# Constant products on TensorE before the first tile, sums moved from VectorE to GpSimd, and gate copies placed elsewhere, in a two-block model on one core

## What is computed

```
def even_layer(h, ...):
    q, k, v, g_a, z, xbc, dt_raw = split(h @ w_in)
    y_a = rmsnorm(diff_attention(q, k, v), subln_w) * 0.8 * silu(g_a)
    xs, bm, cm = split(silu(causal_dwconv(xbc, conv_w, conv_b)))
    y = ssd_scan(xs, softplus(dt_raw + dt_bias), A, bm, cm) + xs * d_skip
    y_b = group_rmsnorm(y * silu(z), ssd_norm_w)
    return concatenate([y_a, y_b]) @ w_out

def _hybrid_mixer(u, ...):
    g = sigmoid(g_merge)                       # [.., 3, 1024]
    merged = (g[0] * (o_a @ w_up[0]) + g[1] * (o_b @ w_up[1]) + g[2] * (o_c @ w_up[2]))
    return merged @ w_out
```

## Time and profile before

| | |
|---|---|
| median of three runs | 1611.04 us |
| lowest, highest | 1607.83, 1613.50 us |
| profiled execution, its own time | 1614.3 us |
| its span in the profile | 1612.6 us |
| PE busy | 1551.4 us (96%) |
| DVE, ACT, POOL busy | 810.5, 659.5, 233.9 us |
| mean granted clock of PE | 0.987 |

### The profile page before, as it was taken

One profiled execution on the slowest core, in us unless ns is written; L12 is line 12 of the kernel. 1 busy time (PEld: TensorE's weight loads), 2 busy tenths in 40 slices (PEclk: granted clock), 3 DMA queues, 4 the chain that ended last, 5 costly groups with the idle time before them and its releaser, 6 DMA issues. The chain is left out here.

```text
span 1612.6 us, 20637 instructions
## 1 busy us (share of the span) xinstructions
PE 1551.4 (96%) x7850; PEld 1269.7 (79%) x7850; DVE 810.5 (50%) x1617; ACT 659.5 (41%) x1369; POOL 233.9 (15%) x147
## 2 busy tenths in 40 slices
PE   7999999999999999999999999999899999999998
PEld 6888777777787889878878777778777888888886
DVE  3323288757734566546524476737556333333224
ACT  4222355565523377634225544454245322322112
POOL 0000022155400012200012223122102000000000
PEclk9999999999999999999999999989999999999999
DMA  5232211111322431023521311112220323222232
GB/s 211 91 105 91 92 56 50 53 47 46 118 91 79 141 89 53 28 92 110 155 77 54 105 66 53 53 53 93 90 79 26 105 92 105 91 96 101 91 105 78
DMA packets 39777, 137.60 MB, mean 85 GB/s; under 512 B 4928, under 2 KB 5312, under 8 KB 39552
## 3 DMA queue, kind: packets, MB, share of 16 engines
q1 hardware_dynamic: 33984, 123.75, 22.9%
q10 hardware_dynamic: 5696, 12.55, 2.6%
HBM read 128.02 MB, written 2.10 MB: 81 GB/s over the span
## 5 line engine op out<-in xcount | busy, mean ns | idle before, releaser
L213 ACT ACTIVATE cut_hi<-raw 128x1024 fp32r<-128x1024 f32 x228 | 241.8, 1061 | 603.9 <-PE ps L230 594.2
L230 PE MATMUL ps<-h_hi,cut_hi 128*128 128x512 f32 (+1 forms) x1120 | 450.6, 402 | 10.6 <-DVE arena L1234 6.2
L218 DVE TENSOR_TENSOR cut_lo<-raw,cut_hi 128x1024 fp32r<-128x1024 f32 x171 | 211.3, 1235 | 461.7 <-ACT cut_hi L213 459.9
L232 PE MATMUL ps<-h_hi,cut_lo 128*128 128x512 f32 (+1 forms) x1120 | 437.0, 390 | 0.0
L231 PE MATMUL ps<-h_lo,cut_hi 128*128 128x512 f32 (+1 forms) x1120 | 436.4, 390 | 0.0
L230 PEld LDWEIGHTS ps<-h_hi,cut_hi 128*128 128x128 f32 x1120 | 211.5, 189 | 75.0 <-issue 23.6
L232 PEld LDWEIGHTS ps<-h_hi,cut_lo 128*128 128x128 f32 x1120 | 211.3, 189 | 45.1
L231 PEld LDWEIGHTS ps<-h_lo,cut_hi 128*128 128x128 f32 x1120 | 211.8, 189 | 37.4
L218 POOL TENSOR_TENSOR cut_lo<-raw,cut_hi 128x1024 fp32r<-128x1024 f32 x57 | 137.6, 2414 | 649.6 <-ACT cut_hi L213 649.6
L230 PE MATMUL ps<-cut_hi,h_hi 128*128 128x512 f32 (+1 forms) x304 | 118.3, 389 | 6.4 <-DVE cut_lo L218 5.4
L232 PE MATMUL ps<-cut_hi,h_lo 128*128 128x512 f32 (+1 forms) x304 | 117.4, 386 | 0.0
(11 more groups left out here) (348 smaller groups left out, 2199.8 us busy)
## 6 DMA issues: line engine op xcount, KB each, us to landing
raw<-weights SPq DMA_DIRECT2D x228, 512.0 KB, 3.3
scr<-scr ACTq DMA_DIRECT2D x34, 64.0 KB, 3.5
x<-x_in SPq DMA_DIRECT2D x4, 512.0 KB, 6.3
x<-x_in ACTq DMA_DIRECT2D x1, 2048.0 KB, 7.9
q_stack<-qT_lo ACTq DMA_DIRECT2D x16, 128.0 KB, 2.3
out<-x SPq DMA_DIRECT2D x4, 512.0 KB, 2.6
consts<-tables ACTq DMA_DIRECT2D x1, 1732.0 KB, 7.9
big_row<-big_in ACTq DMA_DIRECT2D x2, 512.0 KB, 7.0
```

The lines of the kernel that those rows point to most:

```text
L213: act.activation(cut_hi[:, u % CUT, :], raw[:, u % RAW, :], ACT.Copy).then_inc(hi_ready, 1)
L218: eng.tensor_tensor(cut_lo[:, u % CUT, :], raw[:, u % RAW, :], cut_hi[:, u % CUT, :].bitcast(F32), ALU.subtract).then_inc(lo_ready, 1)
L230: a = pe.matmul(out, left[0], right[0], start=start, stop=False)
L232: return a, pe.matmul(out, left[1], right[0], start=False, stop=stop)
```

## The change

Eighteen matmuls of a constant tile by itself are put in front of PE's first wait; the tile is set by DVE (the wait counts of `setup_chain` go up by one). In `Norm.dve` each tile is scaled right after its own `add_eps`. In the state-space stage seven of the eight copies of L1234 stand earlier in DVE's program: copy 0 before the copies of x, copy 1 before the scalings by dt, copies 2, 3, 5, 6 before the `mix` of their chunk, copy 7 behind one gating of `out_a` and not three; copy 4 stays. In `Up` POOL makes the last four sums too, DVE cuts the low half of `out_m`'s unit 0 and makes the low halves of tiles 0 to 3 behind the gatings 16 to 19; the high and low halves of tiles 4 to 7 go to `out_m` (new class `OutM`), behind the cuts of its unit 1.

```diff
+        warm = part(0, [P])
+
         class Setup(Part):
+            WARM = 18
...
             def pe(self, pe):
+                pe.wait_ge(setup_chain, 2)
+                for i in range(self.WARM):
+                    pe.matmul(ps[:, i % 8, 0:P], warm[:, 0:P], warm[:, 0:P], start=True, stop=True)
                 pe.wait_ge(const_loaded, 16)
 
             def dve(self, dve):
                 dve.memset(neg_half, -0.5).then_inc(setup_chain, 1)
+                dve.memset(warm, 1.0).then_inc(setup_chain, 1)
...
                 else:
-                    for t in range(self.nt + 1):
-                        if t < self.nt:
-                            self.add_eps(dve, t)
-                        if t:
-                            self.scale(dve, t - 1)
+                    for t in range(self.nt):
+                        self.add_eps(dve, t)
+                        self.scale(dve, t)
...
                 dve.tensor_tensor(pick[:, :], ident[:, 0:64], ident[:, 64:128], ALU.add)
+                gates.dve_turn(dve, 0)
                 for p, i in enumerate(TURN_ORDER):
...
-                    if p == 3:
-                        gates.dve_turn(dve, 0)
...
+                gates.dve_turn(dve, 1)
                 dve.wait_ge(*turn_out(6))
                 dve.wait_ge(*turn_out(7))
                 for t in range(NT - 1):
                     times_dt(dve, t, xdt_ready)
-                gates.dve_turn(dve, 1)
...
+                    if i in (0, 1, 4, 5):
+                        gates.dve_turn(dve, 2 + (0, 1, 2, 4, 5).index(i))
                     if i < 7:
                         mix(i + 1)
...
-                    if i in (0, 1, 2, 4, 5):
-                        gates.dve_turn(dve, 2 + (0, 1, 2, 4, 5).index(i))
+                    if i == 2:
+                        gates.dve_turn(dve, 4)
...
                     if i == 6:
-                        for k in range(3):
+                        out_a.gate(dve, 0)
+                        gates.dve_turn(dve, 7)
+                        for k in range(1, 3):
                             out_a.gate(dve, k)
-                        gates.dve_turn(dve, 7)
...
                 cut_high(act, self.u0 + 6)
-                for j in range(4, 8):
-                    act.wait_ge(up_last, j - 3)
-                    act.activation(h_hi[:, j, :], m_sum[:, j, :], ACT.Copy, scale=0.5).then_inc(merged_hi, 1)
...
-                    if j == 0 and i < 20:
+                    if j == 0:
                         cut_low(dve, self.u0 + i // 4 + 1)
...
-                    if i >= 20:
-                        dve.wait_ge(up_gated, i + 1)
-                        dve.tensor_tensor(m_sum[:, tile, :], m_sum[:, tile, :], m_new[:, j, :], ALU.add)\
-                            .then_inc(up_last, 1)
-                        self.low(dve, i - 20)
-                for j in range(4, 8):
-                    self.low(dve, j)
+                    if 16 <= i < 20:
+                        self.low(dve, i - 16)
...
-                for i in range(20):
+                for i in range(24):
...
-                cut_low(pool, self.u0 + 6)
...
+        class OutM(Combine):
+
+            def act(self, act):
+                cut_high(act, self.u0 + 1)
+                for j in range(4, 8):
+                    act.wait_ge(up_added, 9 + j)
+                    act.activation(h_hi[:, j, :], m_sum[:, j, :], ACT.Copy, scale=0.5).then_inc(merged_hi, 1)
+                for k in range(2, self.nk):
+                    cut_high(act, self.u0 + k)
+
+            def before_sums(self, dve):
+                cut_low(dve, self.u0 + 1)
+                for j in range(4, 8):
+                    self.before.low(dve, j)
+                for k in range(2, self.nk):
+                    cut_low(dve, self.u0 + k)
```

More of the change, by code:

```diff
@@ L346, in dve @@
                 dve.tensor_tensor(scr[:, 64:128], row("lq2"), row("lk2"), ALU.mult).then_inc(setup_chain, 1)
-                dve.wait_ge(setup_chain, 3)
+                dve.wait_ge(setup_chain, 4)
                 dve.tensor_reduce(small[:, 332:333], scr[:, 0:64], AXX, ALU.add).then_inc(lam_dots, 1)
@@ L356, in dve @@
                    .then_inc(setup_chain, 1)
-                dve.wait_ge(setup_chain, 4)
+                dve.wait_ge(setup_chain, 5)
                 dve.tensor_scalar(neg_lam, small[:, 352:353], LAMBDA_INIT, -1.0, ALU.add, ALU.mult)\
@@ L2891, in build @@
                       lambda k: (o_parts[0][:, k, :], o_parts[1][:, k, :]), 6)
-        up_done, up_gated, up_added, up_last, merged_hi, merged_lo = (
-            sem(m) for m in ("up_done", "up_gated", "up_added", "up_last", "merged_hi", "merged_lo"))
+        up_done, up_gated, up_added, merged_hi, merged_lo = (
+            sem(m) for m in ("up_done", "up_gated", "up_added", "merged_hi", "merged_lo"))
         m_sum = scr[:, 0:4096].rearrange("p (j s) -> p j s", j=8)
@@ L2972, in pool @@
                     added += 1
-                cut_low(pool, self.u0 + 6)
         up = Up()
-        out_m = Combine("out_m", "out_m", lambda k: (h_hi[:, k, :], h_lo[:, k, :]), 8, before=up)
+        class OutM(Combine):
[12 more added lines that the diff above has]
+                    cut_low(dve, self.u0 + k)
+        out_m = OutM("out_m", "out_m", lambda k: (h_hi[:, k, :], h_lo[:, k, :]), 8, before=up)
         mem_q = part(11264, [2, S])
```

## The result

The changed kernel's median is 1599.29 us (four runs, 1597.47 to 1601.73), that of the kernel before, run beside it, 1612.27 us (four runs). The ratio is 0.9917, 95% interval 0.9894 to 0.9940: 13 us less, and 1597.4 was forecast. A second, longer comparison on another occasion gave 0.9945 (0.9922 to 0.9967), 9 us less; the two intervals overlap. The profiled execution took 1597.47 us with a span of 1595.8 us.

The account below looks back on a forecast made before the run. PE is busy 1551.4 of 1612.6 us, so only what stands in its way counts. Terms -8.4 - 6.0 - 0.1 + 0.9 = -13.6 take the profiled 1614.3 to 1600.7, less 3.3 for the median: 1597.4; range 1590.5 to 1605.0.

Parts of the forecast that it names:

- State-space stage: Moved gate copies in L1390 to L1585 remove PE's waits and two half-clock stretches: 8.4 us less, bounds 5.0 and 10.7.
- gate 0: State-space stage, copy ahead of four x copies: PE goes on 1.9 us sooner, 1.7 of clock, less 0.2: 3.4 us.
- gate 5: State-space stage, copy moved ahead of a `mix`: wait of 1.82 us at 400.33, 0.2 refill and half-clock stretch go: 3.7.
- rival A: Clock: small PE waits remain and half-clock stretches move instead of going, 5.1 us back: 1602.5 us; chance 0.10.
- Up projection: Both PE waits behind `out_m`'s first unit and 1.7 us of half clock go: 6.0 us less, bounds 6.6 and 2.0.
- Rival B: Up projection, shared port: each of four POOL sums goes ahead of a DVE low half, +4.0: 1601.4 us; chance 0.08.
- Start: Eighteen constant products and `Norm.dve`'s new order at the beginning: 0.1 us gained; bounds 0.9 and 1.7 lost.
- Rival C: Kernel's beginning: PE idles between single tiles and first products run at half clock, 1.7 + 0.1: 1599.2 us; chance 0.07.
- MemoryNorm: It inherits `Norm.dve`'s order, so the second `add_eps` and power stick out: 0.9 us lost, bounds 0.5 and 2.6.
- D: State-space stage: late Tanhs make four moved gate copies hold their `mix` and PE's product, slower: 1620.2 us; chance 0.03.
- E: State-space stage: moved copies wait for something else, only the 6.0 less 0.8 is won: 1605.8 us; chance 0.06.
- gate 1: State-space stage: wait of 1.38 us at 353.69 goes, but PE's next work needs the first `mix`: 0, at most 1.4.

Follow-up runs that it names:

- The gates alone: Kernel before with only the state-space stage's gate copies moved as in the change; ratio to before 0.9954 (0.9937 to 0.9971), -7.4 us.
- the kernel with the filling at 352: Changed kernel plus five unread identity products in PE's wait before the first product of the state-space stage; ratio to before 0.9922 (0.9895 to 0.9949).
- unfilled variants: Versions of the changed kernel without added products in PE's waits; 35 executions, the change included, took 1599.7 us on average.

## Why the prediction was right, point by point

**State-space stage, 8.4 forecast.** Of it 5.0 was waits (1.7 at gate 0, 1.3 at gate 2, 2.0 at gate 5) and 3.4 clock. The gates alone gained 4.7 in their stage: 1.7 at 340.64, as worked out for gate 0. The clock's 3.4 is the step that failed, and it failed as rival A said: half clock moved and didn't go. I read "the clock fell right behind the two longest waits" as cause and effect, from one trace. Over five traces with these waits they bring 6.8 / 5 / 2 = 0.7 us at 339 and 17 / 5 / 2 = 1.7 us at 400; and the wait for the first `mix`, which I had costed at nothing because 1.38 us had done nothing before, brings 27.2 / 7 / 2 = 1.9 us back (27.2: the column at 352 in the seven traces).

**Up projection, 6.0 forecast.** Measured 6.0, alone and in the whole. Low halves beside sums took 1.18 and not 0.68, three times, and unit 0's cut 1.1 us longer: 2.6 where 2.6 was reckoned (2.0 + 0.6), and one wait of 0.45 stayed. That the clock's 1.7 came in full is luck of these traces: behind the 3.64 us it fell in 4 of 5. Rival B would have needed a whole sum ahead of each; a sum was under way for only part of each. On the other side of the port, POOL's four sums beside the early low halves took 6.78 and not 5.04. The Trainium skill ("SBUF — State Buffer", "SBUF: two separate sides") says that the one that starts first then blocks the other for the whole instruction. The traces agree: a low half of 1.18 us is 0.68 and a wait of 0.5 for the rest of a sum, and a sum of 1.7 us is 1.26 and a wait for the rest of a low half.

**Start, 0.1 forecast.** The term was mis-sized: the first high half comes 1.0 to 1.6 us earlier in the seven traces of the change with constants, 1.2 without them, and the order itself is worth 1.1 to 1.2. The step that failed is "POOL's power takes 0.99, so tile 3 is scaled near 14.5". The power took 0.99 only beside a scaling; in the new order no scaling runs then, it takes 0.55, and tile 3 was scaled at 12.25 (12.2 to 12.8 in the eight traces), with only tile 2's transposes ahead of it in PE's queue. Rival C's half clock came in both traces of the change (11 to 16 us) and ended before the first product; in the kernel with the filling at 352 it reached 1.3 us into the products, 0.6 us of time.

**MemoryNorm, 0.9 lost forecast.** 0.65 lost alone, 0.65 in the whole, 0.66 given back when undone. The two powers take 1.37 side by side with the scaling and 0.55 each alone, so less sticks out than the 0.69 I took.

**The sum.** Without the clock the forecast had 8.5 us (5.0 + 4.3 + 0.1 - 0.9); the traces show 4.7 + 4.3 + 1.2 - 0.65 = 9.6 by place, and all executions 10.2. With the clock, 5.1 was forecast at three places. There the traces average 0.7 + 1.7 + 1.4 - 1.9 = 1.9. All half clock together fell in the traces from 43.1 (mean of five with the old waits) to 30.3 us (mean of six with the change and nothing filled), 6.4 us of PE's time, the most of it at 720, 825 and 1045 us, in stages that the change doesn't touch. The other executions don't bear this out: by the clock of each, the change has 1.4 us less half clock than the kernel before, its unfilled variants with it 3.7 less (0.7 to 6.6), so the traces of the old waits happened to lie high and those of the change low. The clearest fall is that of the gates alone, 29.1 us against 36.8 in the kernel before beside them. What sets the total is open.

So the forecast is nearest where it needed the clock least: 8.5 us of places, and 9.6 to 10.2 measured. Its 5.1 us of clock did not come: 0.7 us in the executions of the change. That 13 us less were measured, and 13.6 forecast, is luck in part: all 63 and 11 executions give means 11.0 us apart (9.4 to 12.5), below the forecast, though well inside its range.

Two readings in the prediction are off and change nothing: DVE's low half ended 0.55 us behind POOL's cut (1138.63 + 2.88 = 1141.51 against 1140.96), not 0.47, and the best case is 1593.3 - 3.2 = 1590.1, not 1590.5.

**Rivals.** D and E fell. A came true in part, B not, C with next to no effect.

## What to carry to other kernels

A copy that empties a bank for which PE waits belongs ahead of the steps for which its engine would idle anyway. If the copy then holds a later step, that is harmless as long as PE has other work queued: look how long before its use that step ends. A removed wait is worth its own length where PE's next work is ready (1.7 us at gate 0), and nothing where it isn't (gate 1's 1.38 us came back as 1.33). A half-clock stretch behind it is worth nothing for sure: read the clock in several traces, and in the mean clock of all executions, before pricing it. Where a small operation on GpSimd seems slow, look which VectorE operation stands beside it before taking its time over into the new order.

## What was not expected of the hardware

- The granted clock falls behind the same pause in one execution and not in the next: 1.86 us at 338 us, full clock in three of five traces. Total half clock was 25.7 to 46.5 us over 14 traces, 10 us of PE's time. It makes nearly the whole scatter of the kernel before: 63 executions took 1605.4 to 1617.8 us, the 26 with the least half clock all under 1610 us and the other 37 all above.
- GpSimd's power of one column took 0.55 us alone and 0.99 us beside a VectorE scaling that reads a single tile.
- Eighteen constant products in front raised nothing that lasted: PE idled at 8 to 11 us anyway, and without them the transposes alone reached the full clock, eight in 1.10 us from 11.95 on against sixteen in 3.60 from 7.51 (read from their pace: the profile's clock is 1.00 in both stretches). By the Trainium skill ("TensorE: Matmul & The Clock Gate", Part 4) transposes don't engage the full clock; these traces disagree.
